# Norms of the out and down stages finished bank by bank, the last block's x2 kept in SBUF and its results stored from the SP queue, in a hybrid decoder layer

## The chip, the cores and the metric

The kernel runs on 1 core of one Trainium2 chip. The metric is the device time of one execution in microseconds, lower is better. Three executions of the kernel before took 2289.16, 2289.42 and 2293.85 us; the median is 2289.42.

## The reference

One layer of a decoder trunk, for 2048 prompt tokens and 32 sample tokens (8 requests of 4), width 1024, all in fp32. Cut to what matters here:

```python
def rms_norm(x, g):
    y = x * rsqrt(mean(x * x, axis=-1) + EPS)
    return y * g

h = rms_norm(x, g_mix_pre); z = h @ w_in           # 1024 -> 2048
# four mixers (pooling, conv, gated chunk MLP, short conv) on parts of z
o = concat([y_a, y_b, y_c, y_d]) @ w_out           # 1024 -> 1024
x = x + rms_norm(o, g_mix_post)                    # this is x2
f = rms_norm(x, g_ffn_pre)
f = square(relu(f @ w_up)) @ w_down                # 1024 -> 4096 -> 1024
x = x + rms_norm(f, g_ffn_post)                    # this is y
```

The outputs are y for the prompt and the sample tokens and small states. Each norm needs the sum of squares over all 1024 columns of a token, so it can be finished only when all column panels of that token are there.

## The kernel before, in words

**Arithmetic.** Each fp32 product is three fp32r matmuls (L1695 to L1697): both operands are split into a high part and the rest. For weights, SP loads a panel of 256 columns into `raw`, ScalarE writes `w_hi` (`split_hi`, L635) and VectorE `w_lo` (`split_lo`, L1079). There are two buffers of each, so panel j + 2 is split after panel j has been used.

**Stages.** Phase 1 (input projection and mixers) is not touched. Phase 2 works on four blocks b of 512 tokens, the last with the 32 sample tokens more. `order` lists the weight panels: O (out projection, 4 panels), U (up projection) and D (down projection) in 4 quarters q, each of 4 U panels and 4 D panels. Between blocks the order is D(q=3, p=0) of block b-1, then O p=0 to 3 of block b, then D(q=3, p=1 to 3) of block b-1, then U of block b. So while TensorE does the three last D panels, VectorE and ScalarE turn block b's out projection into the input of its U stage.

**Tiles and banks.** O and D panels compute tokens on the partitions: a tile is 128 tokens x 256 columns, 24 matmuls; two tiles share one PSUM bank (`token_banks`), the sample tile has one of its own. Six banks go round (`mm`). Evictions: `o_copy` (VectorE) into `o_sb`, `d_copy` (ScalarE, q = 0) and `d_add` (VectorE, q > 0) into `f2_sb`. After an eviction ScalarE takes the sum of squares of each tile's 256 columns (`o_squares`, `y_squares`, L863 and L931) into one column of `oms` or `yms`.

**From o to f.** When all four O panels of a block are there, `o_inverse` on VectorE sums the four columns for all of the block's tiles (L1384), ScalarE takes the root (`o_root_of`, L869), VectorE the reciprocal (L1386). Then tile by tile: `x2_tile` (L1395, L1399: scale, add x from `x_in`), `x2_stat` on ScalarE (L879, L881), `f_tile` (L1405, L1409), `transpose_f` on TensorE (L1921, eight transposes into the two banks `tr`), `f_part` on ScalarE (L889, `act_hi`) and on VectorE (L1417, `act_lo`). `transpose_f(b, i)` waits until both engines' `f_part(b, i - 1)` have read the same bank. The order of these on each engine, mixed with `split_hi`, `split_lo`, `d_add` and `y_squares` of the D panels, is written out by hand: `f_of_first` for block 0, `f_between` for the others, one of each on ScalarE and on VectorE. TensorE's places for the transposes are written in its own loop: behind tile (p, tile) = (1, 3), (2, 1), (2, 3), (3, 1) and, for the sample tile, (3, 3) of the D panels. In block 0 all four stand behind the last O panel.

**From down to y.** `y_inverse` (L1455, L1457), `y_root_of` (L937) and `y_tile` (L1465, L1469) do the same for y. For blocks 0 to 2 they are spread over the next block's first four U panels; for the last block they stand behind everything. x2 is written to DRAM by POOL (L614) and read back by POOL (`rows_in`, L555) into the two buffers `x_in`; POOL also stores y (`results`, L563). Each load of x2 into a buffer waits for the `y_ready` of the tile two before.

## Time and profile before

| | |
|---|---|
| profiled execution | 2289.91 us, span of its instructions 2288.1 us |
| median of the runs | 2289.42 us (2289.16 to 2293.85) |
| mean granted TensorE clock | 0.977 |
| ScalarE busy | 752.6 us (33%) |
| GpSimd busy | 115.0 us (5%) |
| weight split L1079, VectorE | 152 of 2292 ns mean |
| weight split L635, ScalarE | 152 of 1913 ns mean |
| stores of x2, POOL's queue | 16 of 512 KB and one of 128 KB |
| loads of x2 from DRAM | 16 of 512 KB and one of 128 KB |

The busy shares are over the whole span. A share does not say what a stage is limited by, so the rows below go by stage: where TensorE waits, and what the other engines do then. A row of a timeline gives the start, the duration, the engine, the line, the operation and its operands, and in brackets how long the engine sat idle before it and for what.

### The profile page before, as it was taken

The page shows a single profiled execution, that of the slowest core. Times are in us where ns is not written, and L with a number is a line of the kernel's source. Part 1 is how long each engine was busy: PE and PEld are TensorE (multiplying, and loading weights), DVE is VectorE, ACT ScalarE, POOL GpSimd, SP SyncE. Part 2 cuts the span into 40 slices and gives each one's busy share as a digit, 9 for nine tenths or more (in the row PEclk, how much of TensorE's full clock was granted, in tenths as well). Part 3 has the DMA queues.
Part 4 walks back from the last instruction along what each step waited for, and adds up shares of the span by engine and source line. Part 5 has one row for each costly group of instructions (what it writes and reads, how often), then busy time and mean ns, then how long its engine had stood idle before and what let it go on. Part 6 is the DMA issues. An engine that isn't in the chain of part 4 may idle for free.

```text
span 2288.1 us, 32980 instructions
## 1 busy us (share of the span) xinstructions
PE 2147.0 (94%) x14425; PEld 1945.0 (85%) x14425; DVE 1081.4 (47%) x1388; ACT 752.6 (33%) x1145; POOL 115.0 (5%) x205
## 2 busy tenths in 40 slices
PE   6989997979699999999999999999999989999996
PEld 4877775768488988988898899889898989999996
DVE  3677766775643333465333346533334553334243
ACT  4233232224333223443323244332324442313131
POOL 2000110010000000000000000000000000000000
PEclk9999998989799999999999999999999999999998
DMA  6754644553232223445233334533223434222221
GB/s 211 242 212 170 212 169 170 180 192 103 102 112 93 93 93 102 131 154 166 93 99 99 98 130 148 166 100 102 93 93 119 137 115 135 85 83 78 90 74 60
DMA packets 186084, 291.87 MB, mean 128 GB/s; under 512 B 6128, under 2 KB 162453, under 8 KB 177733
## 3 DMA queue, kind: packets, MB, share of 16 engines
q1 hardware_dynamic: 160997, 168.64, 23.2%
q0 software_dynamic: 24656, 120.96, 15.0%
q8 instruction: 114, 1.87, 0.3%
q14 instruction: 30, 0.24, 0.0%
q10 hardware_dynamic: 287, 0.16, 0.0%
HBM read 247.24 MB, written 42.80 MB: 127 GB/s over the span
## 4 chain that ended last, share of the span: by engine, by line
PE 66%; issue 18%; DVE 7%; ACT 4%; DMA 3%; ACTq 0%; POOL 0%; SPq 0%; POOLq 0%; DVEq 0%
PE mm L1695 21%; PE mm L1696 21%; PE mm L1697 21%; ACT w_hi L635 2%; DVE w_lo L1079 2%; DVE conv L1122 2%; DMA mixc<-mixT_scratch 1%; DMA x_in<-in_x_prompt 1%; PE tr L1700 1%; PE tr L1729 1%; DMA raw<-in_w_in 1%; PE tr L1921 0%; DVE o_sb L1399 0%; PE mm L1756 0%; DVE conv_s L1606 0%
## 5 line engine op out<-in xcount | busy, mean ns | idle before, releaser
L1079 DVE TENSOR_TENSOR w_lo<-raw,w_hi 128x2048 fp32r<-128x2048 f32 x152 | 348.4, 2292 | 707.1 <-ACT w_hi L635 707.1
L1695 PE MATMUL mm<-act_hi,w_hi 128*128 128x512 f32 (+1 forms) x1728 | 638.5, 369 | 9.8 <-DVE act_lo L1417 6.0
L1696 PE MATMUL mm<-act_lo,w_hi 128*128 128x512 f32 (+1 forms) x1728 | 632.6, 366 | 0.0
L1697 PE MATMUL mm<-act_hi,w_lo 128*128 128x512 f32 (+1 forms) x1728 | 630.0, 365 | 0.0
L1695 PE MATMUL mm<-w_hi,u_hi 128*128 128x256 f32 (+1 forms) x2176 | 603.3, 277 | 1.5
L1697 PE MATMUL mm<-w_hi,u_lo 128*128 128x256 f32 (+1 forms) x2176 | 601.0, 276 | 0.0
L1696 PE MATMUL mm<-w_lo,u_hi 128*128 128x256 f32 (+1 forms) x2176 | 600.9, 276 | 0.0
L635 ACT ACTIVATE w_hi<-raw 128x2048 fp32r<-128x2048 f32 x152 | 290.8, 1913 | 582.0 <-PE mm L1697 581.1
L1695 PEld LDWEIGHTS mm<-w_hi,u_hi 128*128 128x128 f32 (+1 forms) x2176 | 398.3, 183 | 4.8 <-DVE u_lo L1433 3.6
L1696 PEld LDWEIGHTS mm<-w_lo,u_hi 128*128 128x128 f32 (+1 forms) x2176 | 398.3, 183 | 1.2
L1697 PEld LDWEIGHTS mm<-w_hi,u_lo 128*128 128x128 f32 (+1 forms) x2176 | 398.3, 183 | 0.7
L1695 PEld LDWEIGHTS mm<-act_hi,w_hi 128*128 128x128 f32 x1728 | 327.4, 189 | 68.8 <-issue 13.4
L1697 PEld LDWEIGHTS mm<-act_hi,w_lo 128*128 128x128 f32 x1728 | 327.1, 189 | 56.3
L1696 PEld LDWEIGHTS mm<-act_lo,w_hi 128*128 128x128 f32 x1728 | 327.1, 189 | 55.2 <-issue 2.4
L1695 PE MATMUL mm<-w_hi,act_hi 128*128 128x256 f32 (+1 forms) x736 | 210.3, 286 | 17.7 <-DVE act_lo L1365 14.9
L1697 PE MATMUL mm<-w_hi,act_lo 128*128 128x256 f32 (+1 forms) x736 | 208.2, 283 | 0.0
L1696 PE MATMUL mm<-w_lo,act_hi 128*128 128x256 f32 (+1 forms) x736 | 208.0, 283 | 0.0
L904 ACT ACTIVATE square<-mm 128x512 f32<-128x512 f32 (+1 forms) x160 | 81.8, 511 | 262.5 <-PE mm L1697 262.5
L1122 DVE SCALAR_TENSOR_TENSOR conv<-g_ext,cst,conv 128x512 f32<-128x512 f32 x240 | 162.6, 745 | 0.7 <-ACT conv L739 0.7
L1695 PEld LDWEIGHTS mm<-w_hi,act_hi 128*128 128x128 f32 (+1 forms) x736 | 133.7, 182 | 20.2 <-issue 15.5
L1431 DVE CAST u_hi<-square 128x512 fp32r<-128x512 f32 (+1 forms) x160 | 59.9, 374 | 192.3 <-ACT square L906 192.3
L1696 PEld LDWEIGHTS mm<-w_lo,act_hi 128*128 128x128 f32 (+1 forms) x736 | 133.3, 181 | 2.2 <-issue 0.5
(238 smaller groups left out, 1350.4 us busy)
## 6 DMA issues: line engine op xcount, KB each, us to landing
raw<-in_w_ffn_up SPq DMA_DIRECT2D x64, 1024.0 KB, 5.4
raw<-in_w_ffn_down SPq DMA_DIRECT2D x64, 1024.0 KB, 5.1
w_hi<-whi_scratch POOLq DMA_DIRECT2D x24, 1024.0 KB, 5.2
w_lo<-wlo_scratch POOLq DMA_DIRECT2D x24, 1024.0 KB, 7.9
raw<-in_w_out SPq DMA_DIRECT2D x16, 1024.0 KB, 5.3
raw<-in_w_in SPq DMA_DIRECT2D x8, 1024.0 KB, 9.5
whi_scratch<-w_hi POOLq DMA_DIRECT2D x8, 1024.0 KB, 8.7
wlo_scratch<-w_lo POOLq DMA_DIRECT2D x8, 1024.0 KB, 10.7
```

The costliest lines, as they stand in the source:

```text
L635: SC.activation(w_hi[:, s, :, :], raw[:, s, :, :], ACT.Copy).then_inc(hi_ready, 1)
L904: SC.activation(square[:, at % 2, 0:c1 - c0], mm[bank][:, 0:c1 - c0], ACT.Relu).then_inc(bank_free[bank], 1)
L1079: DVE.tensor_tensor(w_lo[:, s, :, :], raw[:, s, :, :], w_hi[:, s, :, :].bitcast(fp32), ALU.subtract)\
L1122: DVE.scalar_tensor_tensor(out=c, in0=g_ext[:, t, k:k + N1], scalar=col("conv_w", 2 * k + t), in1=c, op0=ALU.mult, op1=ALU.add).then_inc(c ...
L1431: DVE.tensor_copy(u_hi[:, k, c0:c1], square[:, at % 2, 0:c1 - c0]).then_inc(u_hi_ready, 1)
L1695: PE.matmul(out, whi, xhi, start=(k == 0), stop=False)
L1696: PE.matmul(out, whi, xlo, start=False, stop=False)
L1697: return PE.matmul(out, wlo, xhi, start=False, stop=(k == K - 1))
L1700: PE.matmul(bank[:, 0:n], headmean[:, :], src, start=True, stop=True).then_inc(done, 1)
L1729: last = PE.transpose(tr[hh][:, kk * P:(kk + 1) * P], x_tile(n)[:, k * P:(k + 1) * P], ident[:, :])
```

## The change

1. The norms of the out stage (`o_inverse`, `o_root_of`) and of the down stage (`y_inverse`, `y_root_of`) are done per PSUM bank g, that is for two token tiles at a time and the sample tile by itself: two rounds per block, three in the last.
2. The eviction of the last O panel is taken into `f_of_first` and `f_between`: bank 0 is copied and squared, its norm and x2_tile(0) and (1) follow, then bank 1. The splits of panels j + 2 are moved behind that, and the order of the rest is written anew. `last_o_panel` is gone.
3. TensorE's places for the f transposes in the D panels become (1, 3), (2, 0), (2, 3), (3, 0) and (3, 1).
4. In the last block x2 stays in `o_sb`: no store, no reload. The last D panel is evicted bank by bank, and each bank's norm, y tiles and stores follow at once.
5. The last block's y is stored by SP.

```diff
+        def span(b, g):
+            tiles = token_banks(b)[g]
+            return tiles[0][0], tiles[-1][0] + 1
...
@@ SP
+            for i, _, n in tiles_of(NB - 1):
+                sp.wait_ge(y_ready, no(NB - 1, i) + 1)
+                sp.dma_start(y_rows(NB - 1, i, n), f2_sb[0:n, i, :]).then_inc(y_last, 16)
+            sp.wait_ge(y_last, 16 * NT)
             sp.wait_ge(out_small, 16 * OUT_SMALL)
-            sp.wait_ge(y_out, 16 * (NCH * NB + 1))
+            sp.wait_ge(y_out, 16 * NCH * (NB - 1))
@@ POOL
-                    pool.wait_ge(x2_ready, no(b, i) + 1)
-                    pool.dma_start(x2_d[...], o_sb[0:n, i, :]).then_inc(x2_out, 16)
+                    if b < NB - 1:
+                        pool.wait_ge(x2_ready, no(b, i) + 1)
+                        pool.dma_start(x2_d[...], o_sb[0:n, i, :]).then_inc(x2_out, 16)
...
-            results(NB - 1)
@@ ScalarE
             def f_of_first():
-                o_root_of(0)
-                for i in range(3):
-                    x2_stat(0, i)
+                j = J2 + NP - 1
+                o_squares(j, 0)
+                o_root_of(0, 0)
+                x2_stat(0, 0)
+                x2_stat(0, 1)
+                o_squares(j, 1)
+                o_root_of(0, 1)
+                split_hi(j + 2)
+                x2_stat(0, 2)
                 f_part(0, 0)
                 x2_stat(0, 3)
                 for i in range(1, NCH):
                     f_part(0, i)
...
             def f_between(b):          # the new order, whole
                 o_squares(j1 - 1, 0);  o_root_of(b, 0);  x2_stat(b, 0);  x2_stat(b, 1)
                 o_squares(j1 - 1, 1);  if tail: o_squares(j1 - 1, 2)
                 split_hi(j1 + 1);  o_root_of(b, 1);  if tail: o_root_of(b, 2)
                 x2_stat(b, 2);  y_squares(j1, 0);  split_hi(j1 + 2)
                 x2_stat(b, 3);  if tail: x2_stat(b, NCH)
                 y_squares(j1, 1);  f_part(b, 0);  f_part(b, 1);  y_squares(j1 + 1, 0)
                 f_part(b, 2);  split_hi(j1 + 3);  y_squares(j1 + 1, 1)
                 f_part(b, 3);  if tail: f_part(b, NCH)
                 y_squares(j1 + 2, 0);  split_hi(j1 + 4);  y_squares(j1 + 2, 1)
...
+                    elif b == NB - 1:
+                        for p in range(NP - 1):
+                            token_panel(index("D", b, q, p), d_piece)
+                        for g in range(3):
+                            y_squares(NPAN - 1, g)
+                            y_root_of(b, g)
@@ VectorE
+            def o_inverse(b, g):
+                a, e = span(b, g)
+                dve.wait_ge(o_sq, NP * no(b, 0) + (NP - 1) * len(tiles_of(b)) + e)
+                DVE.tensor_reduce(osum[:, a:e], oms[:, a:e, :], AX.X, ALU.add).then_inc(o_sum, 1)
+                dve.wait_ge(o_root, 2 * b + g + 1)
+                DVE.reciprocal(oinv[:, a:e], oroot[:, a:e]).then_inc(o_inv, 1)
...
             def y_tile(b, i):
+                    x2 = o_sb[0:n, i, :]      # last block only
...
             def f_of_first():          # the new order, whole
                 o_copy(j, 0);  o_inverse(0, 0);  x2_tile(0, 0);  x2_tile(0, 1);  o_copy(j, 1)
                 f_tile(0, 0);  o_inverse(0, 1);  f_tile(0, 1);  x2_tile(0, 2);  f_part(0, 0)
                 x2_tile(0, 3);  f_part(0, 1);  f_tile(0, 2);  f_tile(0, 3);  f_part(0, 2)
                 f_part(0, 3);  split_lo(j + 2)
             def f_between(b):          # the new order, whole
                 o_copy(j1 - 1, 0);  o_inverse(b, 0);  x2_tile(b, 0);  x2_tile(b, 1)
                 o_copy(j1 - 1, 1);  if tail: o_copy(j1 - 1, 2)
                 split_lo(j1 + 1);  o_inverse(b, 1);  if tail: o_inverse(b, 2)
                 f_tile(b, 0);  f_tile(b, 1);  x2_tile(b, 2);  d_add(j1, 0);  x2_tile(b, 3)
                 split_lo(j1 + 2);  if tail: x2_tile(b, NCH)
                 d_add(j1, 1);  f_part(b, 0);  f_tile(b, 2);  f_part(b, 1);  f_tile(b, 3)
                 d_add(j1 + 1, 0);  f_part(b, 2);  if tail: f_tile(b, NCH)
                 split_lo(j1 + 3);  d_add(j1 + 1, 1);  f_part(b, 3);  if tail: f_part(b, NCH)
                 d_add(j1 + 2, 0);  split_lo(j1 + 4);  d_add(j1 + 2, 1)
...
+                        for g in range(3):
+                            d_add(NPAN - 1, g)
+                            y_inverse(b, g)
+                            for i in range(*span(b, g)):
+                                y_tile(b, i)
@@ TensorE
-                                if (p, tile) == (2, 1):
+                                if (p, tile) == (2, 0):
                                     transpose_f(b + 1, 1)
                                 if (p, tile) == (2, 3):
                                     transpose_f(b + 1, 2)
-                                if (p, tile) == (3, 1):
+                                if (p, tile) == (3, 0):
                                     transpose_f(b + 1, 3)
-                                if (p, tile) == (3, 3) and b == NB - 2:
+                                if (p, tile) == (3, 1) and b == NB - 2:
                                     transpose_f(b + 1, NCH)
```

j1 is panel D(p=1), so j1 - 1 is the last O panel, j1 + 1 is D(p=2), j1 + 2 is D(p=3), j1 + 3 and j1 + 4 are the next block's first two U panels; `tail` is true for the last block.

## Rows read from the trace of the kernel before

**Rows 1.** Page, busy us by engine (share of span) and instructions.

```profile
PE 2147.0 (94%) x14425; PEld 1945.0 (85%) x14425; DVE 1081.4 (47%) x1388; ACT 752.6 (33%) x1145; POOL 115.0 (5%) x205
```

**Rows 2.** TensorE's waits, whole span: total us, times, longest.

```profile
PE tr L1921 <- DVE f_sb L1409: 20.9, 5, 15.6
PE tr L1921 <- DVE act_lo L1417: 14.8, 8, 5.2
PE mm L1695 <- DVE act_lo L1417: 6.0, 2, 4.4
```

**Rows 3.** Timeline of TensorE ahead of block 0's U stage.

```profile
583.11 1.97 PE L1921 MATMUL tr<-ident,f_sb 128*128 128x128 f32 x8 [15.58 <-DVE f_sb L1409]
...
602.15 0.77 PE L1695 MATMUL mm<-act_hi,w_hi 128*128 128x512 f32 x1 [1.61 <-DVE act_lo L1417]
```

**Rows 4.** Timeline of TensorE, first U matmul of block 3.

```profile
1853.60 0.56 PE L1695 MATMUL mm<-act_hi,w_hi 128*128 128x272 f32 x1 [4.41 <-DVE act_lo L1417]
```

**Rows 5.** Timeline of VectorE at the end.

```profile
2258.53 0.69 DVE L1449 TENSOR_TENSOR f_sb<-mm,f_sb 128x512 f32<-128x512 f32 x1 [5.03 <-PE mm L1697]
...
2266.69 0.41 DVE L1449 TENSOR_TENSOR f_sb<-mm,f_sb 32x256 f32<-32x256 f32 x1 [2.03 <-PE mm L1697]
...
2268.44 1.29 DVE L1465 SCALAR_TENSOR_TENSOR f_sb<-f_sb,yinv,g_out 128x1024 f32<-128x1024 f32 x1
...
2276.87 1.23 DVE L1469 TENSOR_TENSOR f_sb<-f_sb,x_in 128x1024 f32<-128x1024 f32 x1 [2.23 <-DMA x_in<-x_scratch]
...
2282.42 1.21 DVE L1469 TENSOR_TENSOR f_sb<-f_sb,x_in 32x1024 f32<-32x1024 f32 x1
```

**Rows 6.** Timeline of POOL at the end: the last store's issue.

```profile
2283.92 0.50 POOL L563 DMA_DIRECT2D out<-f_sb  x1 [1.86 <-DVE f_sb L1469]
```

**Rows 7.** Timeline of VectorE in block 1's f_between.

```profile
970.49 0.69 DVE L1378 COPY o_sb<-mm 128x512 f32<-128x512 f32 x1 [0.70 <-PE mm L1697]
...
978.11 2.29 DVE L1079 TENSOR_TENSOR w_lo<-raw,w_hi 128x2048 fp32r<-128x2048 f32 x1 [1.32 <-ACT w_hi L635]
...
982.38 1.22 DVE L1399 TENSOR_TENSOR o_sb<-o_sb,x_in 128x1024 f32<-128x1024 f32 x1
...
995.07 1.29 DVE L1417 TENSOR_TENSOR act_lo<-tr,act_hi 128x512 fp32r<-128x512 f32 x2 [0.21 <-ACT act_hi L889]
```

**Rows 8.** Timeline of ScalarE in the same stretch.

```profile
971.22 0.42 ACT L863 ACTIVATE junk_o<-o_sb 128x256 bf16<-128x256 f32 x1 [0.34 <-DVE o_sb L1378]
...
976.15 1.92 ACT L635 ACTIVATE w_hi<-raw 128x2048 fp32r<-128x2048 f32 x1 [3.88 <-PE mm L1697]
...
979.03 1.28 ACT L869 ACT_TABLE_LOAD   x1
980.51 0.30 ACT L869 ACTIVATE oroot<-osum,eps 128x4 f32<-128x4 f32 x1 [0.20 <-DVE osum L1384]
983.64 1.06 ACT L879 ACTIVATE junk<-o_sb 128x1024 bf16<-128x1024 f32 x1 [2.83 <-DVE o_sb L1399]
...
994.46 1.06 ACT L889 ACTIVATE act_hi<-tr 128x512 fp32r<-128x512 f32 x2
```

**Rows 9.** Timeline of TensorE in the same stretch, the transposes that waited.

```profile
988.11 1.09 PE L1921 MATMUL tr<-ident,f_sb 128*128 128x128 f32 x8 [1.16 <-DVE f_sb L1409]
...
995.90 1.22 PE L1921 MATMUL tr<-ident,f_sb 128*128 128x128 f32 x8 [1.24 <-DVE act_lo L1417]
...
1009.98 1.23 PE L1921 MATMUL tr<-ident,f_sb 128*128 128x128 f32 x8 [0.68 <-DVE act_lo L1417]
```

**Rows 10.** Windows: length, busy by engine, granted clock, DMA share, GB/s.

```profile
570.00:571.00 1.00, 0.00 (x0) 0.00 (x0) 1.00 (x3) 0.17 (x1) 0.35 (x1) 0.93 0.00 0
...
605.00:606.00 1.00, 1.00 (x6) 0.82 (x5) 0.00 (x0) 0.00 (x0) 0.00 (x0) 1.00 0.00 0
...
970.00:978.00 8.00, 8.00 (x71) 8.00 (x71) 1.38 (x2) 3.71 (x10) 0.00 (x0) 1.00 0.41 133
...
1857.00:1858.00 1.00, 1.00 (x7) 1.00 (x7) 0.00 (x0) 0.00 (x0) 0.00 (x0) 0.66 0.00 0
```

More of the change, by code:

```diff
@@ L360, in hybrid_trunk_step @@
         y_out = sem("y_out")
+        y_last = sem("y_last")
         OUT_SMALL = 2 + 3 * NB_S + 1 + 3
@@ L1047, in _ @@
                         if b > 0 and q == 0 and p == 0:
-                            y_root_of(b - 1)
+                            for g in range(2):
+                                y_root_of(b - 1, g)
                         if b == 0 and q == 0:
@@ L1491, in d_piece @@
                     d_add(j, i)
-            def last_o_panel(j):
-                _, b, q, p = order[j]
-                for i in range(len(token_banks(b))):
-                    o_copy(j, i)
-                split_lo(j + 2)
             def f_of_first():
-                o_inverse(0)
+                j = J2 + NP - 1
+                o_copy(j, 0)
+                o_inverse(0, 0)
                 x2_tile(0, 0)
                 x2_tile(0, 1)
+                o_copy(j, 1)
                 f_tile(0, 0)
+                o_inverse(0, 1)
+                f_tile(0, 1)
                 x2_tile(0, 2)
-                f_tile(0, 1)
                 f_part(0, 0)
                 x2_tile(0, 3)
+                f_part(0, 1)
                 f_tile(0, 2)
-                f_part(0, 1)
                 f_tile(0, 3)
@@ L1513, in f_of_first @@
                 f_part(0, 3)
+                split_lo(j + 2)
             def f_between(b):
@@ L1518, in f_between @@
                 tail = len(tiles_of(b)) > NCH
-                o_inverse(b)
+                o_copy(j1 - 1, 0)
+                o_inverse(b, 0)
                 x2_tile(b, 0)
                 x2_tile(b, 1)
+                o_copy(j1 - 1, 1)
+                if tail:
+                    o_copy(j1 - 1, 2)
+                split_lo(j1 + 1)
+                o_inverse(b, 1)
+                if tail:
+                    o_inverse(b, 2)
+                f_tile(b, 0)
+                f_tile(b, 1)
+                x2_tile(b, 2)
                 d_add(j1, 0)
-                f_tile(b, 0)
-                x2_tile(b, 2)
+                x2_tile(b, 3)
                 split_lo(j1 + 2)
+                if tail:
+                    x2_tile(b, NCH)
                 d_add(j1, 1)
-                f_tile(b, 1)
                 f_part(b, 0)
-                x2_tile(b, 3)
-                d_add(j1 + 1, 0)
                 f_tile(b, 2)
                 f_part(b, 1)
+                f_tile(b, 3)
+                d_add(j1 + 1, 0)
+                f_part(b, 2)
+                if tail:
+                    f_tile(b, NCH)
                 split_lo(j1 + 3)
                 d_add(j1 + 1, 1)
-                f_tile(b, 3)
-                f_part(b, 2)
-                if tail:
-                    x2_tile(b, NCH)
-                d_add(j1 + 2, 0)
                 f_part(b, 3)
                 if tail:
-                    f_tile(b, NCH)
+                    f_part(b, NCH)
+                d_add(j1 + 2, 0)
                 split_lo(j1 + 4)
                 d_add(j1 + 2, 1)
-                if tail:
-                    f_part(b, NCH)
             b = NB - 1
@@ L1658, in _ @@
                             if p == 0:
-                                y_inverse(b - 1)
+                                for g in range(2):
+                                    y_inverse(b - 1, g)
                             y_tile(b - 1, p)
@@ L1683, in _ @@
                             token_panel(j + 1 + p, o_copy)
-                        last_o_panel(j + NP)
                         f_between(b + 1)
-            y_inverse(NB - 1)
-            for i in range(len(tiles_of(NB - 1))):
-                y_tile(NB - 1, i)
         @block.tensor
```

88 lines of the change are left out of this document (46 added, 42 removed).

## The prediction, made before the changed kernel ran

> **What bounds the kernel now.** I read the shares by engine first: TensorE is busy 94% of the span [rows 1]. So the change can help only where TensorE stands still or after its last matmul, and it can hurt only where it makes TensorE stand. Next I read TensorE's own waits. Those that this change touches are the waits of the f transposes (L1921) and of the first up-projection matmuls for the normalised x2: 20.9 us in 5 waits of the transposes for `f_tile`, 14.8 us in 8 for `f_part`, and 6.0 us in 2 of those matmuls [rows 2]. The largest, 15.6 us, is in the stretch ahead of block 0's MLP [rows 3]; the rest lies in the three `f_between` stretches, some 3.1 us in each of the first two and some 9.4 us in the last (4.41 us of it at its end [rows 4]). Then the end: VectorE's last `d_add`s, one norm over five tiles, ten big VectorE operations, with stalls for reloaded x2, and the store [rows 5, 6]. The four stretches and the end are worked out one by one below, from durations and orders of the code: each engine takes its instructions in order, and about 0.04 us passes from a release to the start of the next.
>
> **The end (gain).** Before: the last bank (32 tokens) is evicted at 2266.7, the norm is ready at 2268.44, the last addition ends at 2282.42 + 1.21 = 2283.63, and the store follows at 2283.92; the span ends at 2288.1, that is 4.5 us after the last y [rows 5, 6]. After: bank 0 is evicted at 2258.53 + 0.69 as before. Then two squares on ScalarE (0.54 each) and the norm's three small operations: for the last bank 2266.69 to 2268.44 is 1.75, of which 0.4 is the eviction and 0.6 its square, so the norm is 0.75 [rows 5]. y_tile(0) starts at 2261.1. A tile is its scaling (1.29 [rows 5]) and its addition (1.22 [rows 7]), with their small overlap 2.46 us of VectorE, so tiles 0 and 1 end at 2266.0. Bank 1 (done by 2264) is evicted by 2266.7, squares and norm take 1.9, y_tile(2) starts at 2268.7, tile 3 ends at 2273.6; bank 2: eviction 0.4, squares 0.6, norm 0.8, tile 2.5: y at 2278.0. With the same 4.5 us behind it the end is 2282.5: **5.6 us less**. Three norms instead of one cost 1.9 us of it; that x2 is in SBUF removes the 2.23 us stall [rows 5] and a smaller one of 0.7. The store now goes out on SP, where nothing but the final waits is behind it; no row shows a small store on that queue. Bounds: nothing is issued faster (POOL's 0.5 us issue is 4.5 us from the end anyway), so the gain is 4.6 to 6.6. The Trainium skill (DMA: Bandwidth & Descriptors, the table at its head and "SWDGE vs HWDGE vs iDMA") gives about 1 us to the first byte for a DMA issued by GpSimd and 0.6 us for one from SP; by it the end would come 0.4 us earlier still, an estimate from that page, and no run here shows it yet.
>
> **f_of_first (block 0).** Before, `o_copy`(bank 0) starts at 570.1 behind `conv_out`; this does not change. After, the first norm no longer waits for the weight split (`split_lo` 2.29, `split_hi` 1.92 [rows 7, 8]); it waits for two squares, a table load of 1.28 and the root, so x2_tile(0) starts at 573.8 against 576.7. That lead is given back. The second norm makes VectorE wait for ScalarE (1.1 us), `split_hi` and x2_stat(2) stand ahead of f_part(0) on ScalarE, and f_tile(2) is now behind f_part(1), which waits for x2_stat(3). f_tile(2) is done at 596.6 against 594.7. Transposes of tile 2 at 596.7 (596.0 before), first U matmul at 602.5 against 602.15 [rows 3]: **+0.4 us**, bounds -1 and +2.
>
> **f_between of blocks 1 and 2 (loss).** This decides. The transposes of tile 1 are moved from behind tile 1 to behind tile 0 of panel D(p=2), and `transpose_f(b, 1)` needs the two PSUM banks `tr`, which are free only when both ScalarE's and VectorE's f_part(0) are done. Before, f_part(0) on VectorE ran at 995.07 [rows 7] and TensorE waited 1.24 us [rows 9]. After, f_part(0) is behind more work on both engines. For block 1, with the last O panel's bank 0 copied at 970.49 as now [rows 7]:
> squares 971.22 to 972.3, table load 1.28 to 973.6, root 0.30, reciprocal [rows 8]: x2_tile(0) at 974.1, x2_tile(1) ends 979.1 (2 x 2.46), o_copy(bank 1) to 979.7. ScalarE: x2_stat(1) (1.06 + 0.19 + 0.29 with overlap, 1.4) to 980.6, squares of bank 1 to 981.6, `split_hi` 1.92 to 983.55. VectorE stands from 979.7 to 983.6 for it, then `split_lo` 2.29, the second norm 0.77, f_tile(0) at 986.6 to 988.04, f_tile(1) to 989.4, x2_tile(2) to 991.9, d_add, x2_tile(3) to 995.0. ScalarE: x2_stat(2) to 993.3, y squares to 994.4, `split_hi` to 996.3; VectorE: `split_lo` to 998.6, d_add(D1, bank 1) to 999.24; ScalarE: its squares to 1000.36, f_part(0) to 1001.0; VectorE f_part(0) 1001.00 to 1001.7. The transposes of tile 1 start at **1001.7**.
> TensorE: f(0) transposed at 988.1 as before (0.98 us), then tile 0 of D(p=2): 24 matmuls at 8.00/71 = 0.113 us [rows 10] are 2.72. It is at the transposes of tile 1 at 991.8 and **stands 9.9 us**. Work that used to cover f_part(0) (tile 1) is now behind the wait, and so is everything else on TensorE. After that nothing is late: f_tile(2) to f_tile(3) are done during the three tiles behind it, so the waits of 1.24 and 0.68 [rows 9] and some 0.3 us go. Net +9.95 - 2.2 = **+7.7 us** for block 1. Block 2 has no table load there, so f_tile(0) comes 1 us earlier and its wait, 1.16 in block 1 [rows 9], shrinks to 0.35; the stall is the same 9.95, since both ends move together: **+6.7 us**.
> That the wait is this long turns on two round trips that are now ahead of f_part(0) on both engines, x2_tile(3) with its statistic, and `split_hi`/`split_lo` with d_add(D1, bank 1) and its squares. Bounds for one stall: 7.5 (both engines overlap better than in order) to 11.
>
> **f_between of block 3.** The same chain plus a third norm (0.8), one more square, x2_tile(4) (2.5) and its statistic ahead of f_part(0): stall 12.1. The waits before (9.4 measured, 10.3 by the same working) go down to 2.0 for the transposes of the sample tile, now at (3, 1) and so covered by two more tiles; the 4.41 us wait of the first U matmul [rows 4] goes. Net 12.1 + 2.4 - 10.3 = **+4.3 us**.
>
> **The clock.** TensorE stopped at 583.11 - 15.58 = 567.53; the granted clock fell from 1.00 to 0.50 (2.4 to 1.2 GHz) within the stretch 570 to 571, which has 0.93 [rows 3, 10]. It worked again from 602.15 and had 1.00 by 605 to 606; in block 3 it worked from 1853.60 and came back in 1857 to 1858 (0.66) [rows 4, 10]. So a stop of 10 us ends at half clock, and half of the following 2.9 to 4.1 us is lost: 1.4 to 2.0. In blocks 1 and 2, which lose nothing now, 1.7 each: **+3.4 us**. In block 3 the loss moves from U to D: 0.
>
> **Small edits.** Two norms instead of one for the earlier blocks' y: some 0.8 us of VectorE and ScalarE waits inside the U panels, covered by 11 us of matmuls per panel (VectorE busy 47% [rows 1]); if not, 1 us a block. Five stores and five loads less on POOL: off TensorE's path. The tighter weight split (w_lo of D(p=2) at 985.9, TensorE there at 986.9) holds by 1 us; missed, it takes the place of the f(0) wait.
>
> **Sum.** 7.7 + 6.7 + 4.3 + 3.4 + 0.4 - 5.6 = +16.9 us on the profiled execution's 2289.91 (span 2288.1): 2306.8. The median shown is 0.5 lower: **2306.3**. The same working, applied to the order of before, puts the first U matmuls of blocks 0 and 3 at 602.11 and 1853.04, where the trace has 602.15 and 1853.60 [rows 3, 4]: its own error is some 0.5 us a stretch.
>
> **Rivals.** (A) The reordering does what its names say: f(1) is ready 6 us earlier (989.4 against 995), and no f wait is left in the three stretches. Then the 15.5 us of waits in them (20.9 + 14.8 + 6.0 less block 0's 15.6, 9.0 and 1.6) and block 3's 2 us of clock go, and the end's 5.6: 2289.4 - 23 = 2266. It is decided at one place: f_part(0) must be done before TensorE has tile 0 of D(p=2), 991.8. Against it: two `split` pairs are ahead of it. Chance 0.05. (B) The stall is there, but part of it is covered (7.5 each) or the clock costs nothing: 2306.3 - 3 x 2.4 = 2299, or 2302.9. Chance 0.17. (C) A second wait behind the stall: the split of U's weights, `split_hi`(U0) now behind f_part(2) on ScalarE, or the sample tile's transposes, 2 us in each of three stretches: 2312. For it: ScalarE and VectorE hand over ten times in each stretch; against it: f_part(3) is ready 3 us ahead. Chance 0.14. (D) Between A and B, a stall of some 4 us, time within 0.2%: 0.03. The forecast itself (2303 to 2309): 0.61.
>
> **How the numbers follow.** A difference of 0.2%, 4.6 us, is about what can be told from no change. Faster: A, 0.05. Same: 0.03. Slower: the forecast, B and C, 0.92. The range 2299 to 2312 takes in B's and C's prices and leaves out A and D.
>
> **What would show it.** A wait of some 10 us of the L1921 transposes for act_lo (f_part) in each of three stretches, 30 us in total in place of the small ones of [rows 2]; granted clock 0.50 at its end; f_part(0) of block 1 near 1001 on VectorE; three short reduces at the end and the last y 11 us after TensorE's last matmul, not 17; no reload of x2 at the end. It is wrong if f_part(0) runs before 992 or if TensorE's new wait is under 5 us.

## The result: 13 us slower

The changed kernel takes 2303.88 us (median of 4 runs, 2302.48 to 2304.13) against 2290.74 (2289.16 to 2293.85) for the kernel before, run beside it: ratio 1.0054, 95% interval 1.0037 to 1.0072. The forecast was 2306.3, range 2299 to 2312, worked out on a median of 2289.42: +16.9 us forecast, +13.1 measured. The profiled execution took 2303.94 us, its span 2302.2, mean granted clock 0.972 (0.977 before).

The page's first part after, to be held against [rows 1]: no engine got more work of note. TensorE is busy 4 us more in all, with the same 14425 instructions: the lower clock.

```profile
PE 2151.0 (93%) x14425; PEld 1951.4 (85%) x14425; DVE 1085.3 (47%) x1408; ACT 755.6 (33%) x1155; POOL 107.1 (5%) x190
```

TensorE's waits of the changed kernel, as in [rows 2] (total us, times, longest). `tr` waiting for `act_lo`, a transposition that waits for `f_part`, has gone from 14.8 us in 8 waits to 38.2 in 6:

```profile
PE tr L1965 <- DVE act_lo L1447: 38.2, 6, 11.3
PE tr L1965 <- DVE f_sb L1439: 19.9, 3, 13.2
PE mm L1739 <- DVE act_lo L1447: 1.6, 1, 1.6
```

The timeline of TensorE after: the f transposes of blocks 1, 2 and 3 that waited, and the first U matmul of blocks 0 to 3.

```profile
601.54 0.77 PE L1739 MATMUL mm<-act_hi,w_hi 128*128 128x512 f32 x1 [1.65 <-DVE act_lo L1447]
...
988.28 1.09 PE L1965 MATMUL tr<-ident,f_sb 128*128 128x128 f32 x8 [0.93 <-DVE f_sb L1439]
...
1001.68 1.94 PE L1965 MATMUL tr<-ident,f_sb 128*128 128x128 f32 x8 [9.56 <-DVE act_lo L1447]
...
1026.12 0.40 PE L1739 MATMUL mm<-act_hi,w_hi 128*128 128x512 f32 x1
...
1419.70 1.94 PE L1965 MATMUL tr<-ident,f_sb 128*128 128x128 f32 x8 [9.56 <-DVE act_lo L1447]
...
1443.38 0.40 PE L1739 MATMUL mm<-act_hi,w_hi 128*128 128x512 f32 x1
...
1849.12 1.94 PE L1965 MATMUL tr<-ident,f_sb 128*128 128x128 f32 x8 [11.25 <-DVE act_lo L1447]
...
1877.69 0.29 PE L1739 MATMUL mm<-act_hi,w_hi 128*128 128x272 f32 x1
```

Three stalls, 30.4 us together. The one of block 1 answers to the 1.24 us wait of [rows 9]: the same transposes, of token tile 1, stood at 995.90 there. Each has eight transposes of 1.94 us behind it where an undisturbed group takes 1.09: the clock is at half. Windows of the stretch (length, busy of PE, PEld, DVE, ACT, POOL with instruction counts, granted clock, DMA share, GB/s):

```profile
996.00:997.00 1.00, 0.00 (x0) 0.00 (x0) 0.65 (x1) 1.00 (x2) 1.00 (x2) 0.95 0.48 193
1001.00:1002.00 1.00, 0.32 (x2) 0.35 (x3) 1.00 (x2) 0.30 (x1) 0.00 (x0) 0.50 0.93 310
1006.00:1007.00 1.00, 1.00 (x6) 1.00 (x6) 0.37 (x1) 0.00 (x0) 0.00 (x0) 0.50 0.00 0
1007.00:1008.00 1.00, 1.00 (x10) 1.00 (x9) 0.00 (x0) 0.00 (x0) 0.00 (x0) 0.93 0.00 0
```

TensorE stopped at 992.12 (1001.68 less 9.56), the clock fell from 2.4 to 1.2 GHz at about 997, and came back only at 1007.1, 5.5 us after the restart.

Why it stood is read on VectorE in the same stretch, against [rows 7]. The last row is `f_part(0)` on VectorE; 995.07 before, 1000.85 after. Ahead of it stand two weight splits and `d_add(D1, bank 1)` (L1479), and VectorE waits three times for ScalarE, 6.5 us in all:

```profile
983.82 2.29 DVE L1108 TENSOR_TENSOR w_lo<-raw,w_hi 128x2048 fp32r<-128x2048 f32 x1 [3.70 <-ACT w_hi L644]
...
996.35 2.29 DVE L1108 TENSOR_TENSOR w_lo<-raw,w_hi 128x2048 fp32r<-128x2048 f32 x1 [1.23 <-ACT w_hi L644]
998.56 0.68 DVE L1479 TENSOR_TENSOR f_sb<-mm,f_sb 128x512 f32<-128x512 f32 x1
1000.85 1.29 DVE L1447 TENSOR_TENSOR act_lo<-tr,act_hi 128x512 fp32r<-128x512 f32 x2 [1.60 <-ACT act_hi L899]
```

The two splits alone are not what is new. The kernel before had both of them (978.11 in [rows 7] and 990.57) and the same `d_add` (992.77) ahead of `f_part(0)` too, and waited for ScalarE 1.9 us there; `x2_tile(3)` came behind `f_part(0)`. Its VectorE:

```profile
990.57 2.29 DVE L1079 TENSOR_TENSOR w_lo<-raw,w_hi 128x2048 fp32r<-128x2048 f32 x1
...
996.27 1.28 DVE L1395 SCALAR_TENSOR_TENSOR o_sb<-o_sb,oinv,g_mix 128x1024 f32<-128x1024 f32 x1
```

From the copy of the last O panel's bank 0 (970.49 before, 970.90 after) to `f_part(0)` it is 24.58 us before and 29.95 after. The 5.4 us more are `x2_tile(3)` (2.5), the small operations of the second norm (some 0.4) and 2.5 us more in which VectorE stands. So the wait grew from 1.24 to 9.56 us by 2.7 for the place, one tile of 24 matmuls earlier, and by 5.4 for the order; 0.2 are small shifts.

At the end of the kernel, TensorE's last matmul and VectorE's last operations. [Rows 5] had all ten norm operations behind one root; here a scaling starts 2.54 us after the start of the first eviction, and the last y (2298.63 + 1.21) is done 11.3 us after the last matmul, where it had been 17.3. Both are counted from the start of that matmul.

```profile
2288.51 0.28 PE L1741 MATMUL mm<-w_hi,u_lo 128*32 128x256 f32 x1
```

```profile
2280.73 0.69 DVE L1479 TENSOR_TENSOR f_sb<-mm,f_sb 128x512 f32<-128x512 f32 x1 [5.03 <-PE mm L1741]
...
2283.27 1.28 DVE L1500 SCALAR_TENSOR_TENSOR f_sb<-f_sb,yinv,g_out 128x1024 f32<-128x1024 f32 x1
...
2290.71 1.28 DVE L1500 SCALAR_TENSOR_TENSOR f_sb<-f_sb,yinv,g_out 128x1024 f32<-128x1024 f32 x1
...
2295.63 0.41 DVE L1479 TENSOR_TENSOR f_sb<-mm,f_sb 32x256 f32<-32x256 f32 x1
...
2298.63 1.21 DVE L1503 TENSOR_TENSOR f_sb<-f_sb,o_sb 32x1024 f32<-32x1024 f32 x1
```

**Where the time went.** The span is cut at the start of the first U matmul of each block (U1 is block 1's) and at the start of the last matmul. Spans are read to 0.1 us, so the column "to the end" and its differences hold to 0.05. The table is that ledger, for the kernel before and for every kernel that ran (us, profiled execution):

| kernel | first U | to U1 | to U2 | to U3 | to last matmul | to the end | span | median |
|---|---|---|---|---|---|---|---|---|
| before | 602.15 | 414.36 | 409.53 | 427.56 | 412.71 | 21.79 | 2288.1 | 2290.74 |
| after | 601.54 | 424.58 | 417.26 | 434.31 | 410.82 | 13.69 | 2302.2 | 2303.88 |
| e1, old places | 603.70 | 420.69 | 413.75 | 428.34 | 410.90 | 13.72 | 2291.1 | 2291.73 |
| e2, old f_between | 603.39 | 415.30 | 410.03 | 429.22 | 413.05 | 13.71 | 2284.7 | 2286.08 |
| e3, f_part(0) early | 599.57 | 413.88 | 408.08 | 425.82 | 410.81 | 13.74 | 2271.9 | 2275.58 |
| e4, old order, new places | 601.34 | 421.73 | 419.48 | 446.31 | 412.62 | 13.72 | 2315.2 | 2318.21 |
| e5, stores on POOL | 602.89 | 422.56 | 416.48 | 434.46 | 410.82 | 15.39 | 2302.6 | 2304.18 |
| e6, one norm at the end | 599.15 | 425.08 | 416.56 | 434.38 | 410.82 | 16.81 | 2302.8 | 2305.39 |
| e7, e3 and a new first stage | 595.95 | 413.26 | 407.20 | 425.96 | 410.82 | 13.71 | 2266.9 | 2271.38 |
| e8, e7 and a new f_between | 595.85 | 414.15 | 405.42 | 417.57 | 410.82 | 13.69 | 2257.5 | 2257.62 |
| e9, x2 through DRAM | 602.26 | 423.05 | 416.81 | 434.16 | 410.82 | 13.70 | 2300.8 | 2302.95 |

After less before: -0.6, +10.2, +7.7, +6.8, -1.9, -8.1, sum +14.1. The three f_between stretches lose 24.7 us and give back the 1.9 that before lost to the clock behind U3; the end gives 8.1. The first column also moves by up to 4.5 us between kernels whose code up to there is the same (599.15 to 603.70 over after, e1 to e6 and e9), so a median alone doesn't show a difference of 2 us here. Two of the later columns do: over after, e5, e6 and e9, whose code is the same up to the end, the interval to U2 moves by 0.8 us and the one to U3 by 0.3. The interval to U1 moves by 2.5 (422.56 to 425.08), and the granted clock says why. In block 0's U stage TensorE stands 2.4 us for `conv_s`, in every kernel of the table. Behind it the clock stayed at 2.4 GHz in most of them; in after and e6 it was at 1.2 GHz for 3.4 us and in e8 for 6.8, which costs half of that. After's window is below; the same window of e9 has 1.00. The clock's return behind block 0's first U matmul differs too, after 2.8 us in after and up to 5.8 in e6.

```profile
641.00:646.00 5.00, 5.00 (x16) 3.90 (x16) 3.49 (x6) 0.35 (x2) 0.00 (x0) 0.66 0.32 92
```

### The profile page after: what moved, and what is told of

It reads as the page before. It is cut to its first block, busy times and chain, and to the rows that moved or that the text cites. A ratio compares the mean times of both kernels' runs of the same rounds, so it can differ in the third digit from the quotient of the medians.

```text
span 2302.2 us, 32989 instructions
## 1 busy us (share of the span) xinstructions
PE 2151.0 (93%) x14425; PEld 1951.4 (85%) x14425; DVE 1085.3 (47%) x1408; ACT 755.6 (33%) x1155; POOL 107.1 (5%) x190
## 4 chain that ended last, share of the span: by engine, by line
PE 82%; DVE 8%; ACT 5%; issue 3%; DMA 2%; ACTq 0%; SPq 0%; POOL 0%; POOLq 0%; DVEq 0%
PE mm L1739 27%; PE mm L1740 26%; PE mm L1741 26%; DVE conv L1151 2%; ACT w_hi L644 1%; DVE w_lo L1108 1%; DMA mixc<-mixT_scratch 1%; DVE o_sb L1425 1%; PE tr L1744 1%; PE tr L1965 1%; PE tr L1773 1%; DVE o_sb L1429 1%; DMA raw<-in_w_in 1%; ACT junk L889 1%; ACT junk_y L941 0%
```

## The experiments

Theory T: TensorE stands because `f_part(0)` comes late in the new order on ScalarE and VectorE, where tile 3's x2 and statistic and a second norm are now ahead of it beside the two weight splits, while the transposes that wait for it are placed one tile earlier. Rival P: the place alone does it. The end and the first stage have questions of their own.

**e1_old_places: the order new, TensorE's places as before.**

```
-                                if (p, tile) == (2, 0):
+                                if (p, tile) == (2, 1):
                                     transpose_f(b + 1, 1)
...
-                                if (p, tile) == (3, 0):
+                                if (p, tile) == (3, 1):
                                     transpose_f(b + 1, 3)
-                                if (p, tile) == (3, 1) and b == NB - 2:
+                                if (p, tile) == (3, 3) and b == NB - 2:
                                     transpose_f(b + 1, NCH)
```

> The changed kernel with TensorE's places for the f transposes as before: (2, 1), (3, 1), (3, 3). Theory T (f_part(0) comes late because of the new order on ScalarE and VectorE, and the place only decides how many tiles run ahead of the wait): f_part(0) stays at 1000.9, the stall of 9.56 us in blocks 1 and 2 shrinks by the one tile of 2.72 us now ahead of it, to 6.8, in block 3 from 11.3 to 8.5; TensorE reaches U 2.7 us earlier in blocks 1 and 2 and some 4 us earlier in block 3: 2303.9 - 9.5 = 2294. Rival P (the early place alone makes the stall, because tile 1 no longer covers f_part): the stall falls to 1 to 2 us, the time to some 2281.

Measured: 2291.73 us, ratio to before 1.0007 (0.9997 to 1.0016). The stall is not gone; it is one tile of D shorter, as the transposes of tile 1 in block 1 show (timeline of TensorE in e1):

```profile
1003.10 1.94 PE L1965 MATMUL tr<-ident,f_sb 128*128 128x128 f32 x8 [6.85 <-DVE act_lo L1447]
```

9.56 less 6.85 is 2.71, the 24 matmuls of a tile. P would have had the small waits of before. In block 1 the interval is 3.9 shorter than after: 2.7 by the stall, 0.5 because full clock is back 4.5 us after the restart and not 5.5 (window of e1 below, its clock 0.68), 1.7 because the 3.4 us of half clock behind `conv_s` are missing, less 0.9 because full clock came 1.8 us later behind block 0's first U matmul.

```profile
1007.00:1008.00 1.00, 1.00 (x8) 1.00 (x8) 1.00 (x2) 0.00 (x0) 0.00 (x0) 0.68 0.00 0
```

Over the three intervals the old places give back 13.4 of the 24.7 us; 11.3 stay with the new order. Some 0.8 of the 13.4 is the clock in block 0, which the places don't touch.

**e2_old_between: f_between's order on both engines and the places as before; the rest of the change kept.** The norm's reduce, root and reciprocal are still done once for each bank, in a row.

```
             def f_between(b):
...
+                split_lo(j1 + 1)
+                for g in range(len(token_banks(b))):
+                    o_inverse(b, g)
                 x2_tile(b, 0)
                 x2_tile(b, 1)
...
                 d_add(j1, 1)
+                f_tile(b, 1)
                 f_part(b, 0)
+                x2_tile(b, 3)
...
```

> The changed kernel with f_between's order on ScalarE and VectorE and TensorE's places as before; norms still bank by bank, the new f_of_first and the new end stay. Theory T (all of the loss is in f_between, the end gains by itself): waits back to 3 us in blocks 1 and 2 and 9 to 11 us in block 3 (two and three norms in a row, 0.75 us each extra); the end keeps its 13.7 us after the last matmul against 21.8; 2290.7 - 8 + 1 = 2283. Rival Q (the end's gain or f_of_first's change depends on the rest, or the loss sits elsewhere, in the U panels' doubled y norm): over 2288.

Measured: 2286.08 us, ratio 0.9983 (0.9973 to 0.9992): the change without its f_between is a little faster than before, by its end. The 24.7 us of the three stretches are 3.1 here (415.30, 410.03, 429.22 against 414.36, 409.53, 427.56). So they belong to f_between, its order and its places, and not to the finer norms themselves: with the old order the intervals grow by 0.9, 0.5 and 1.7 us. That is the most that the extra rounds of reduce, root and reciprocal can cost. In block 3 TensorE's waits grew by only 0.1 us in sum, and most of the 1.7 is 3.4 us of half clock around 1823, which the kernel before doesn't have there.

**e3_fpart0_early: one call moved on each engine.** Everything else is the changed kernel.

```
                     o_root_of(b, 2)
+                f_part(b, 0)
                 x2_stat(b, 2)
...
                 y_squares(j1, 1)
-                f_part(b, 0)
                 f_part(b, 1)
...
                 d_add(j1, 0)
+                f_part(b, 0)
                 x2_tile(b, 3)
...
                 d_add(j1, 1)
-                f_part(b, 0)
                 f_tile(b, 2)
```

> The changed kernel with one thing moved in f_between: f_part(b, 0) on ScalarE stands right behind the last o_root_of, ahead of x2_stat(b, 2), and on VectorE right behind d_add(j1, 0), ahead of x2_tile(b, 3). Places as changed. Theory T: f_part(0) on VectorE starts at 992.6 in block 1 instead of 1000.9, the wait at (2, 0) falls from 9.56 to 1 to 1.5 us, the granted clock stays at 1.00, and in block 3 the wait at (2, 0) is gone with 2.5 and 3.4 us left for tiles 2 and the sample tile: 7.9 + 7.9 + 6.4 of waits and 2 to 2.7 us of clock in each of blocks 1 and 2 less: 2303.9 - 27 = 2277, and 2281 if the clock gives back nothing. Rival P (the place (2, 0) is too early for any order of this kind, since something else behind the stall, as split_lo of D(p=3), is as late): over 2295.

Measured: 2275.58 us, ratio to before 0.9939 (0.9924 to 0.9953). Timeline of VectorE in e3: `f_part(0)` of block 1 now runs at 990.19, before the second split, where it was at 1000.85.

```profile
990.19 1.28 DVE L1447 TENSOR_TENSOR act_lo<-tr,act_hi 128x512 fp32r<-128x512 f32 x2
...
993.97 2.29 DVE L1108 TENSOR_TENSOR w_lo<-raw,w_hi 128x2048 fp32r<-128x2048 f32 x1
```

TensorE in e3, the same transposes, and the window around them:

```profile
991.02 1.23 PE L1965 MATMUL tr<-ident,f_sb 128*128 128x128 f32 x8 [1.30 <-DVE act_lo L1447]
```

```profile
990.00:1000.00 10.00, 8.98 (x78) 8.83 (x79) 9.63 (x13) 7.32 (x17) 2.09 (x4) 1.00 0.57 203
```

The stall of 9.56 is 1.30, and the clock stays at 2.4 GHz there. The span is 30.3 us shorter than after; 28.4 of it is in the three intervals (10.7, 9.2, 8.5) and 2 in the first column, which this edit doesn't touch. This is the step on which the forecast rested, shown by itself: `f_part(0)` moved up on both engines is worth some 28 us, with the places of the change kept (0.8 of the 28.4 is the clock in block 0). On VectorE it passes `x2_tile(3)`, a weight split and a `d_add`; on ScalarE the statistics of tiles 2 and 3, a split and the squares of D1. Which of these counts most was not run.

**e4_old_order_new_places: e2 with the change's places.** If the place alone did the harm, this would be no worse than the changed kernel.

```
-                                if (p, tile) == (2, 1):
+                                if (p, tile) == (2, 0):
                                     transpose_f(b + 1, 1)
...
-                                if (p, tile) == (3, 1):
+                                if (p, tile) == (3, 0):
                                     transpose_f(b + 1, 3)
-                                if (p, tile) == (3, 3) and b == NB - 2:
+                                if (p, tile) == (3, 1) and b == NB - 2:
                                     transpose_f(b + 1, NCH)
```

> As e2_old_between (order on ScalarE and VectorE as before, new end), but with the changed places (2, 0), (3, 0), (3, 1). Theory T: the places cost by themselves: in blocks 1 and 2 the wait for tile 1 becomes 4.1 us and that for tile 3 3.7 us, together 5.5 us more than in e2 per block, and 11 us more in block 3, where the sample tile's transposes are asked for 5 tiles early: e2 + 22 = 2305, with the clock up to 2309. Rival R (the order is all that counts, places nothing): as e2, 2283.

Measured: 2318.21 us, ratio 1.0125 (1.0110 to 1.0140), the slowest of all. The direction is T's, the size was too low: the intervals are 6.4, 9.5 and 17.1 above e2's, where 5.5, 5.5 and 11 were expected. TensorE's waits in e4:

```profile
PE tr L1957 <- DVE f_sb L1436: 30.3, 6, 13.2
PE tr L1957 <- DVE act_lo L1444: 27.0, 7, 6.0
PE mm L1731 <- DVE act_lo L1444: 8.6, 2, 7.0
```

against e2's

```profile
PE tr L1957 <- DVE f_sb L1436: 27.1, 6, 13.2
PE tr L1957 <- DVE act_lo L1444: 10.3, 6, 6.0
PE mm L1731 <- DVE act_lo L1444: 6.1, 2, 4.4
```

The three lines grew by 22.4 us (65.9 less 43.5), and the three intervals by 33.0. The rest is the clock. The sums of the windows over the three intervals, e4's and then e2's:

```profile
sum 1287.52, PE 1242.31 PEld 1130.21 DVE 533.15 ACT 432.62 POOL 35.29; mean PE 414.10 PEld 376.74 DVE 177.72 ACT 144.21 POOL 11.76
sum 1254.55, PE 1230.62 PEld 1117.11 DVE 532.62 ACT 432.21 POOL 35.28; mean PE 410.21 PEld 372.37 DVE 177.54 ACT 144.07 POOL 11.76
```

TensorE is idle for 45.2 us against 23.9, which is 21.3 more, and is busy 11.7 us longer with the same matmuls: the granted clock was at half for 38 us of these intervals in e4 and for 9 in e2. Groups of transposes that follow a short wait take 1.94 us in e4 (timeline of its TensorE, block 1).

```profile
1012.57 1.94 PE L1957 MATMUL tr<-ident,f_sb 128*128 128x128 f32 x8 [3.69 <-DVE act_lo L1444]
```

So places and order don't add: the places cost 33 us on the old order and 13.4 on the new one (after less e1).

**e7_first_reordered: e3, and f_of_first in another order.** In block 0's stretch there are 34.6 us before, and 35.1 after and in e3, between TensorE's last O matmul and its first U matmul, with only transposes in them. The chain there is the two engines' hand-overs, so the second bank's squares and copy go ahead, and `f_part(0)` ahead of the split on ScalarE.

```
                 o_root_of(0, 0)
+                o_squares(j, 1)
                 x2_stat(0, 0)
                 x2_stat(0, 1)
-                o_squares(j, 1)
                 o_root_of(0, 1)
+                f_part(0, 0)
                 split_hi(j + 2)
                 x2_stat(0, 2)
-                f_part(0, 0)
+                f_part(0, 1)
...
                 o_copy(j, 0)
+                o_copy(j, 1)
                 o_inverse(0, 0)
...
-                f_part(0, 1)
                 f_tile(0, 2)
+                f_part(0, 1)
```

> e3_fpart0_early with f_of_first reordered: on ScalarE f_part(0, 0) right behind o_root_of(0, 1), ahead of split_hi and x2_stat(0, 2), and each f_part(i) ahead of the next x2_stat; on VectorE o_copy(bank 1) ahead of the first norm and f_tile(2), f_tile(3) each ahead of f_part(1), f_part(2). Theory T (the 35 us from the last O matmul to the first U matmul are a chain of hand-overs between VectorE and ScalarE, shortened by order alone): f_part(0) ends 2.5 us earlier, tile 2 is transposed at 592 instead of 596, the first U matmul comes 5.5 us earlier: 2275.6 - 5.5 = 2270. Rival (VectorE's own work or the load of x rows bounds the stretch): under 1.5 us.

Measured: 2271.38 us, ratio 0.9909 (0.9894 to 0.9924). The gap is 29.09 us against 35.07, 6.0 shorter.

**e8_planned_between: e7, and f_between written out anew for all three stretches,** with `f_part(i)` as early as its inputs allow, the weight splits where TensorE leaves room for them, and the transposes placed to suit. The code shows ScalarE's list for blocks 1 and 2 in part; VectorE's is new too, and block 3 has lists of its own.

```
+                    o_squares(j1 - 1, 0)
+                    o_root_of(b, 0)
+                    split_hi(j1 + 1)
+                    x2_stat(b, 0)
+                    o_squares(j1 - 1, 1)
+                    o_root_of(b, 1)
+                    x2_stat(b, 1)
+                    f_part(b, 0)
+                    split_hi(j1 + 2)
...
+                                spots = [(1, 3), (2, 1), (2, 3), (3, 0)] if b + 1 < NB - 1 else [(1, 2), (2, 0), (2, 1), (2, 2), (3, 2)]
```

> e7_first_reordered with f_between written anew from durations of the trace, one list for blocks 1 and 2 and one for block 3: each f_part as soon as both engines can, splits only just ahead of their panel, the squares and d_adds of the D panels late; TensorE's places (1, 3), (2, 1), (2, 3), (3, 0) and, in block 3, (1, 2), (2, 0), (2, 1), (2, 2), (3, 2). Theory T (what is left of TensorE's waits in the three stretches is order alone): waits under 1 us in blocks 1 and 2 against 2.2 and 1.3, none above 1 us in block 3 against 6.2 in sum: first U matmuls 3.3, 2.3 and 7.9 us earlier: e7 - 13 = 2257. Rival (the two engines are at their limit in these stretches, late d_adds and splits come back as waits of the U panels): over 2266.

Measured: 2257.62 us (2255.20 to 2259.36), ratio to before 0.9850 (0.9835 to 0.9864). It is faster than both kernels. Windows of e8 in the last stretch: TensorE has no gap and 2.4 GHz, while VectorE, the engine behind the stall, is busy 8.0 to 9.9 of each 10 us.

```profile
1800.00:1810.00 10.00, 10.00 (x91) 10.00 (x90) 9.89 (x13) 3.99 (x6) 0.51 (x1) 1.00 0.53 160
1810.00:1820.00 10.00, 10.00 (x89) 10.00 (x88) 9.07 (x12) 7.56 (x19) 0.55 (x1) 1.00 0.19 64
1820.00:1830.00 10.00, 10.00 (x93) 9.87 (x91) 7.99 (x9) 5.39 (x12) 0.53 (x1) 1.00 0.64 188
```

Against e7 the intervals are +0.9, -1.8 and -8.4. The first of them is longer although its waits are gone, and that is the clock in block 0, which this edit doesn't touch. Behind the 2.40 us stop for `conv_s` e8 has half clock for 6.8 us (window below; the same window of e7 has 1.00), and behind its first U matmul full clock came 5.8 us later, where it took 3.6 in e7. The two cost 4.5 us.

```profile
634.00:643.00 9.00, 7.31 (x20) 5.96 (x21) 6.09 (x18) 2.77 (x5) 0.00 (x0) 0.62 0.33 109
```

**e5_pool_stores: the last five stores issued by POOL, as before.**

```
-            for i, _, n in tiles_of(NB - 1):
-                sp.wait_ge(y_ready, no(NB - 1, i) + 1)
-                sp.dma_start(y_rows(NB - 1, i, n), f2_sb[0:n, i, :]).then_inc(y_last, 16)
...
+            for i, _, n in tiles_of(NB - 1):
+                pool.wait_ge(y_ready, no(NB - 1, i) + 1)
+                pool.dma_start(y_rows(NB - 1, i, n), f2_sb[0:n, i, :]).then_inc(y_last, 16)
```

> The changed kernel with the last block's five stores issued by POOL instead of SP, all else the same. Theory T1 (the queue makes the 2.1 us by which the end came out shorter than forecast: SP's last y at 2299.84 is 2.4 us before the span's end, POOL's in the kernel before 4.5 us): the stretch from the last matmul to the end grows from 13.7 to 15.8 us, the time by 2 us to 2306. Rival T2 (the shorter tail is the tile order or an emptier DMA queue, not the issuing engine): 13.7 stays, 2304.

Measured: 2304.18 us, ratio 1.0053 (1.0036 to 1.0069): the median can't tell it from the changed kernel, since the first column moves by as much. The ledger can: last matmul to the end is 15.39 against 13.69. VectorE's last operation and POOL's issue in e5:

```profile
2297.33 1.21 DVE L1503 TENSOR_TENSOR f_sb<-f_sb,o_sb 32x1024 f32<-32x1024 f32 x1
```

```profile
2298.83 0.51 POOL L632 DMA_DIRECT2D out<-f_sb  x1 [3.59 <-DVE f_sb L1503]
```

Last y 2298.54, span end 2302.6: 4.0 to 4.1 us. On SP it is 2299.84 to 2302.2: 2.4 us. The queue is worth 1.7.

**e6_one_norm_at_end: one norm over the five tiles, as before; x2 in SBUF and the SP queue kept.**

```
-                            y_inverse(b, g)
-                            for i in range(*span(b, g)):
-                                y_tile(b, i)
...
+                        DVE.reciprocal(yinv[:, 0:NT], yroot[:, 0:NT]).then_inc(y_inv, 1)
...
+                        for i in range(NT):
+                            y_tile(b, i)
```

> The changed kernel with the last block's y norm done once for all five tiles, behind the last d_add, x2 still in SBUF and stores on SP. Theory T1 (per-bank norms buy the time of the four tiles that they let VectorE do under the last matmuls): five tiles of 2.46 us behind the norm, 0.4 + 0.6 + 0.75 + 12.3 + 2.4 us behind the last matmul's end: the stretch is 16.8 instead of 13.7, the time 3 us up, 2307. Rival T2 (x2 in SBUF and the queue are all of the gain): 13.7 stays.

Measured: 2305.39 us, ratio 1.0060 (1.0045 to 1.0075), last matmul to the end 16.81: finishing by bank is worth 3.1 of the 8.1.

**e9_x2_through_dram: the last block's x2 stored and reloaded, as before; norms by bank and SP kept.** The wait for the load stands behind the scaling, as before.

```
-                        x2 = x_in[0:n, at % 2, :]
-                    else:
-                        x2 = o_sb[0:n, i, :]
...
+                at = xin_no["x2", b, i]
+                x2 = x_in[0:n, at % 2, :]
...
+                dve.wait_ge(xin_full[at % 2], 16 * (at // 2 + 1))
```

> The changed kernel with the last block's x2 written to DRAM and read back through x_in as before, while its norms stay bank by bank and its stores on SP. Theory T1 (with the norms by bank the loads have time: x_in for tile 2 is asked for at y_ready(0), 2285.8, and takes some 5.7 us, to 2291.5, before the addition at 2292.0; tile 3 2294.0 before 2294.5): no stall, the stretch from the last matmul to the end stays 13.7 to 14.3 us, and x2 in SBUF is worth under 0.5 us of the 8.1 once the rest is there. Rival T2 (x2 in SBUF is worth what it stalled before, 2.2 + 0.7 us): 16.6 us, the time 2307.

Measured: 2302.95 us, ratio 1.0053 (1.0033 to 1.0073), last matmul to the end 13.70. No addition waits for its load, one row for all five (VectorE, no bracket, where [rows 5] has 2.23 us):

```profile
2290.61 1.23 DVE L1502 TENSOR_TENSOR f_sb<-f_sb,x_in 128x1024 f32<-128x1024 f32 x1
```

## Why the prediction was right, and where its sizes were off

**The stall: right.** Forecast start of the transposes 1001.7, measured 1001.68; stall 9.95, measured 9.56 in both blocks. That the start agrees to 0.02 us is luck: the chain began 0.4 us later than assumed (bank 0 copied at 970.90, not 970.49) and was 0.4 shorter. The cause, that `f_part(0)` comes behind too much on both engines, is shown by e3, and e1 confirms that a tile of D is 2.7 us of it. The reason in words is half right. Of the "two round trips that are now ahead of f_part(0)" only `x2_tile(3)` with its statistic is new; the second split with `d_add(D1, bank 1)` and its squares was ahead of it in the kernel before as well. The working in numbers didn't suffer by it, since it went through every item.

Block 1: forecast 7.7 + 1.7 = 9.4, measured 10.2, of which 1.7 is the half clock behind `conv_s` that no term has. Block 2: 8.4, measured 7.7. The forecast's own terms would give it 0.2 more (7.7 less the 0.8 by which the wait of 1.16 shrinks is 6.9, not 6.7).

**Block 3: 12.1 forecast, 11.25 measured.** Its interval grew by 6.8, and 1.9 came back behind U3, net +4.9 against +4.3. The sample tile's transposes still wait 1.62 us, where 2.0 was forecast; the sum has 2.4 in that place, and 12.1 + 2.4 - 10.3 is 4.2.

**The clock: right in kind, mis-sized one by one.** Full clock was assumed back 2.9 to 4.1 us after a restart. In block 1 it took 5.5 (2.7 us lost against 1.7), in block 2 it took 3.9 (1.9 lost). "In block 3 the loss moves from U to D: 0" is half of it: the 1.9 us behind U3 are gone, and D lost about 2.3 (restart at 1849.12, full clock 4.5 us later), but behind the 1.62 us wait of the sample tile's transposes the clock was at half for another 3.4 us (window 1869 to 1875: 0.72), 1.7 us more. Between the first U matmul and the last matmul TensorE was at half clock for 23.5 us after and for 6.9 before: up to 8.3 us of loss, where the sum has 3.4. The windows after in which the clock came back, of blocks 2 and 3:

```profile
1423.00:1424.00 1.00, 1.00 (x8) 1.00 (x8) 0.96 (x2) 0.00 (x0) 0.00 (x0) 0.72 0.04 13
```

```profile
1853.00:1854.00 1.00, 1.00 (x7) 1.00 (x7) 0.81 (x1) 0.00 (x0) 0.00 (x0) 0.68 0.00 0
```

**The end: the one term that was wrong, -8.1 against -5.6, outside its bounds of 4.6 to 6.6.** Two steps of it failed, and they are separate. First, "with the same 4.5 us behind it": the time from the last y to the end was taken from a store on POOL [rows 5, 6] and used for one on SP, with the reason that nothing is issued faster. It is 2.4 us, and e5 shows the queue as the cause of 1.7 of the 2.1. Of the Trainium skill (DMA: Bandwidth & Descriptors, the table at its head and "SWDGE vs HWDGE vs iDMA") the direction holds, and the estimate of 0.4 us from its figures is a quarter of the 1.7 measured. Second, the reason given for the gain up to the last y. It came out at 6.0 us (17.3 to 11.3), near the forecast, but "that x2 is in SBUF removes the 2.23 us stall" is refuted for this kernel: in e9 x2 is reloaded and nothing stalls. Once the norms go by bank, the additions are spread over the last 15 us and the reloads have time. What each part is worth, from the ledger: norms by bank 3.1 (e6), SP 1.7 (e5), x2 in SBUF on top of these 0 (e9 13.70, after 13.69). Each was undone alone. The other 3.3 belongs to no single one: in e6, with one norm, x2 in SBUF and no reload, the last y is 14.5 us after the last matmul instead of 17.3, so keeping x2 is worth 2.8 there and nothing beside the finer norms. One norm with reloads and the stores on SP was not run.

**f_of_first: +0.4 forecast, +0.44 measured** from the last O matmul to the first U matmul (34.62 to 35.06). That the first U matmul is 0.6 earlier all the same comes from the stages ahead (1.0), which no edit touches.

**The rivals.** A is near to what the change would have been with `f_part(0)` ahead of `x2_tile(3)` and the second split, as in e3, which gains 28 us over after. A's deciding point, the end of tile 0 of D(p=2), was put at 991.8; e3's block 1 runs 2.4 us earlier than after's, and there the point is 989.72 (991.02 less the wait of 1.30), with f_part(0) at 990.19, just behind it. A's price (2266) was 9.6 us better than e3, which keeps 9.8 us of waits in the three stretches, 6.2 of them in block 3. B needed a half-covered stall, C a second wait behind it; neither is there: the U matmuls of blocks 1 and 2 have no wait. The sum: the three stretches were 0.7 above the forecast (22.8 against 22.1), the end 2.5 below it, and the untouched stages 1.0 below, which together is 14.1 of span in place of 16.9. That the three stretches came so near is in part luck. From the first U matmul to the last matmul TensorE is idle 17.4 us more than before, where the terms of the waits add up to 18.7, and loses up to 8.3 to the clock, where the term was 3.4. Together that would be 25.7 of the 22.8 measured: the rest of its work was 2.9 us shorter, which no run explains. And of the four kernels with this code up to there (after, e5, e6, e9) only two show the half clock behind `conv_s`.

**The small edits** cost nothing that the U panels show: the time from block 3's first U matmul to the last matmul is 410.8 to 410.9 in every kernel with the new order, and 412.6 to 413.1 where f_between is the old one (before, e2, e4), where the half-clock loss stands behind that matmul.

## What to carry to other kernels

Where engines take their work in order, read a reordering as a race between one consumer's place and the latest producer on each of two engines: count the hand-overs ahead of it, in the old order as well as in the new, and do it for the buffers that the consumer needs free, not for the data alone. Here a place moved up by one tile and a producer that came 5.4 us later turned a wait of 1.2 us into one of 9.6, and moving the producer alone ahead made the same change 0.6% faster than the kernel before. A gain at the end is priced with its own queue's rows or bounds that admit another queue; and when several edits hide the same stall, undo each alone before giving one the credit.
